# Value pages of four decode samples fetched in turn, their products issued in turn into four 32-column strips

## The reference

```python
k_prev = cache_k[j][page_table].reshape(Bs, PAST_LEN, H_A, DH_A)
v_prev = cache_v[j][page_table].reshape(Bs, PAST_LEN, H_A, DH_A)
...
s = jnp.einsum('bqhd,bqhjkd->bqhjk', qc.astype(F32), kg.astype(F32)) * scale
...
p = jax.nn.softmax(s.reshape(s.shape[:3] + (-1,)), axis=-1).reshape(s.shape)
return jnp.einsum('bqhjk,bqhjkd->bqhd', p, vg.astype(F32)).astype(q.dtype)
```

```python
S = S * g_chunk + jnp.einsum('bjhd,bjhe->bhde', kj * d_out, vj)
...
ob = head_rmsnorm(ob, ret_g) * jax.nn.silu(gb.astype(F32)).reshape(B, T, H_B, DV_B)
```

## Time and profile before

| what | value |
|---|---|
| median of 3 runs | 960.27 us (959.93 to 964.94) |
| span of the profiled execution | 959.2 us |
| PE busy | 883.4 us, 92% |
| DVE busy | 622.1 us, 65% |
| ACT busy | 420.1 us, 44% |
| value pages | 64 DMAs of 256 KB |
| page products (line 1604) | 128 matmul instructions |

### The profile page before, as it was taken

One profiled execution on the slowest core, in us unless ns is written; L12 is line 12 of the kernel. 1 busy time (PEld: TensorE's weight loads), 2 busy tenths in 40 slices (PEclk: granted clock), 3 DMA queues, 4 the chain that ended last, 5 costly groups with the idle time before them and its releaser, 6 DMA issues.

```text
span 959.2 us, 16875 instructions
## 1 busy us (share of the span) xinstructions
PE 883.4 (92%) x6145; PEld 761.0 (79%) x6145; DVE 622.1 (65%) x943; ACT 420.1 (44%) x695; POOL 257.4 (27%) x226
## 2 busy tenths in 40 slices
PE   2999894969999999999999999969969999999996
PEld 1988783742325999999999999857648999999995
DVE  3689988660032798888556656565476888887442
ACT  4434333341011565555545433564334655555442
POOL 6154767710100332232001000161221332222010
PEclk9999996588999999999999999975597999999997
DMA  9837675335565555554556667403353566653631
GB/s 275 284 129 242 199 260 183 128 94 160 192 220 175 176 177 175 178 184 129 172 177 192 191 187 216 161 10 100 88 155 93 171 192 188 188 157 121 183 119 46
DMA packets 154406, 159.83 MB, mean 167 GB/s; under 512 B 11793, under 2 KB 136349, under 8 KB 154335
## 3 DMA queue, kind: packets, MB, share of 16 engines
q1 hardware_dynamic: 145520, 151.09, 50.6%
q10 hardware_dynamic: 7966, 6.33, 2.2%
q0 software_dynamic: 864, 1.68, 0.7%
HBM read 150.76 MB, written 8.50 MB: 166 GB/s over the span
## 4 chain that ended last, share of the span: by engine, by line
PE 81%; DVE 11%; ACT 4%; issue 2%; DMA 2%; ACTq 0%; POOL 0%; SPq 0%; DVEq 0%
PE bank L1396 20%; PE bank L1397 20%; PE bank L1398 20%; PE bank L1604 6%; DVE w_lo L921 3%; DVE sc_all L973 2%; PE bank L1773 1%; PE bank L1726 1%; DMA z<-in_c_out_norm_g 1%; PE bank L1485 1%; PE bank L1600 1%; PE bank L1566 1%; PE bank L1748 1%; PE bank L1737 1%; DVE z L968 1%
## 5 line engine op out<-in xcount | busy, mean ns | idle before, releaser
L530 ACT ACTIVATE w_hi<-w_raw 128x1024 fp32r<-128x1024 f32 (+2 forms) x230 | 227.9, 993 | 297.8 <-PE bank L1398 294.5
L921 DVE TENSOR_TENSOR w_lo<-w_raw,w_hi 128x1024 fp32r<-128x1024 f32 (+2 forms) x230 | 296.1, 1289 | 83.6 <-ACT w_hi L530 83.4
L1396 PE MATMUL bank<-actB_hi,w_hi 128*128 128x264 f32 x704 | 200.1, 284 | 0.0
L1397 PE MATMUL bank<-actB_lo,w_hi 128*128 128x264 f32 x704 | 199.5, 283 | 0.0
L1398 PE MATMUL bank<-actB_hi,w_lo 128*128 128x264 f32 x704 | 199.3, 283 | 0.0
L1396 PE MATMUL bank<-actA_hi,w_hi 128*128 128x264 f32 x624 | 184.8, 296 | 5.8 <-DVE w_lo L921 2.9
L1397 PE MATMUL bank<-actA_lo,w_hi 128*128 128x264 f32 x624 | 180.1, 289 | 0.0
L1398 PE MATMUL bank<-actA_hi,w_lo 128*128 128x264 f32 x624 | 179.8, 288 | 0.0
L1397 PEld LDWEIGHTS bank<-actB_lo,w_hi 128*128 128x128 f32 x704 | 132.6, 188 | 0.1
L1396 PEld LDWEIGHTS bank<-actB_hi,w_hi 128*128 128x128 f32 x704 | 132.6, 188 | 0.1
L1398 PEld LDWEIGHTS bank<-actB_hi,w_lo 128*128 128x128 f32 x704 | 132.0, 187 | 0.0
(11 more groups left out here) (326 smaller groups left out, 1191.2 us busy)
## 6 DMA issues: line engine op xcount, KB each, us to landing
w_raw<-in_ffn_w SPq DMA_DIRECT2D x44, 1024.0 KB, 5.3
kv<-in_cache_k SPq DMA_DIRECT2D x64, 256.0 KB, 3.0
kv<-in_cache_v SPq DMA_DIRECT2D x64, 256.0 KB, 3.1
w_raw<-in_c_w_in SPq DMA_DIRECT2D x16, 1024.0 KB, 5.6
w_raw<-in_ab_w_in SPq DMA_DIRECT2D x14, 1024.0 KB, 5.4
w_raw<-in_ffn_w SPq DMA_DIRECT2D x16, 768.0 KB, 4.5
w_raw<-in_ffn_w SPq DMA_DIRECT2D x16, 640.0 KB, 4.1
w_raw<-in_ab_w_out SPq DMA_DIRECT2D x4, 1024.0 KB, 5.7
```

The costliest lines, as they stand in the source:

```text
L530: A(whi[u % RING][:, 0:nk, :], raw[u // 2 % RING][:, 0:nk, P * (u % 2):P * (u % 2) + P], ACT.Copy).then_inc(sem("hi_ready"), 1)
L921: V.tensor_tensor(wlo[u % RING][:, 0:nk, :], raw[u // 2 % RING][:, 0:nk, P * (u % 2):P * (u % 2) + P], whi[u % RING][:, 0:nk, :].bitcast(F ...
L1396: M(bank[b][:, 0:T], hi[:, k, :], src[0][:, k0 + k, :], start=first and k == 0, stop=False)
L1397: M(bank[b][:, 0:T], hi[:, k, :], src[1][:, k0 + k, :], start=False, stop=False)
```

## The change

The value pages are taken in another order, and SP loads their page numbers pair by pair. `v_page(v)` gives for the v-th fetch the sample, the pair within the sample, and the buffer: fetches 0 to 3 are the first pair of samples 0, 1, 2 and 3, in buffers 0 to 3; fetches 4 to 7 their second pair; from fetch 16 on come samples 4 to 7. PE goes through eight batches of four pairs. In a batch it waits for all four buffers, then issues eight page products, the first page of each of the four samples and then the second of each. Each sample's result lies in its own 32 rows of the bank, as before. The four products for the own token stand together ahead of batches 0 and 4. The retention work moves with `between`: two of its items behind each batch, and the last three behind the last batch.

```diff
--- before.py
+++ after.py
@@ -74,6 +74,11 @@
 JOBS1 = [(n, t, half) for n, t in (("q", 2), ("k", 2), ("v", 2), ("k", 0), ("k", 1), ("v", 0), ("v", 1)) for half in (0, 1)]
 CRING = 3
 EXP_MAX = 41.0
+
+
+def v_page(v):
+
+    return 4 * (v // 16) + v % 4, v // 4 % 4, v % 4
 
 
 def jobs_until(u):
@@ -290,6 +295,19 @@
 
                 page_pair(j, cache_k, (sem("k_reduced"), j - 3) if j >= 4 else None)
 
+            def v_pages(v):
+                b, pair, i = v_page(v)
+                at = NPAGE * b + 2 * pair
+                rows = nc.values_load_multi_w_load_instructions(
+                    pg[0:1, at:at + 2], engines=[mybir.EngineType.SP], min_val=0, max_val=NPOOL - 1)[1]
+                if v < 4:
+                    sp.wait_ge(sem("k_reduced"), 29 + v)
+                else:
+                    sp.wait_ge(sem("v_used"), v - 3)
+                for t in range(2):
+                    sp.dma_start(kv[i][:, t, :], cache_v[0, bass.ds(rows[t], 1)].rearrange("o p h d -> p (o h d)")
+                                 ).then_inc(sem(f"kv_landed{i}"), 16)
+
             for n in range(14):
                 load_raw(n, w_in0[:, :, 256 * n:256 * n + 256])
                 if n == 0:
@@ -310,9 +328,8 @@
                 k_pages(13 + 2 * n)
             for j in range(20, 32):
                 k_pages(j)
-            for j in range(32):
-
-                page_pair(j, cache_v, (sem("k_reduced"), 29 + j) if j < 4 else (sem("v_used"), j - 3))
+            for v in range(32):
+                v_pages(v)
 
             def ffn_loads(l, u_up, u_dn):
                 def pair(n, c, i8):
@@ -1593,22 +1610,31 @@
             claim(7, "samp_own", 2)
             pe.wait_ge(sem("own_p_diag"), 1)
             pe.wait_ge(sem("samp_pt_out"), 1)
-            for j in range(32):
-                b, r = j // 4, 32 * (j // 4 % 4)
-                out = bank[6 + b // 4][r:r + H, :]
-                if j % 4 == 0:
-                    M(out, dgp[:, b, :], tks["va"][:], start=True, stop=False)
-                pe.wait_ge(sem(f"kv_landed{j % 4}"), 32 * (8 + b + 1))
+            def between(n):
+                if n < 4:
+                    state_update(4 + n)
+                elif 5 <= n < 13:
+                    ret_o((n - 5) // 4, (n - 5) % 4)
+                elif 13 <= n < 17:
+                    ret_squares(n - 13)
+
+            for n in range(8):
+                q, pair = n // 4, n % 4
+                outs = [bank[6 + q][32 * i:32 * i + H, :] for i in range(4)]
+                if pair == 0:
+                    for i in range(4):
+                        M(outs[i], dgp[:, 4 * q + i, :], tks["va"][:], start=True, stop=False)
+                for i in range(4):
+                    pe.wait_ge(sem(f"kv_landed{i}"), 32 * (8 + n + 1))
                 for t in range(2):
-                    g = 2 * (j % 4) + t
-                    ins = M(out, pts[:, g, 8 * b:8 * b + 8], kv[j % 4][:, t, :], start=False, stop=g == NPAGE - 1)
-                ins.then_inc(sem("v_used"), 1)
-                if j < 4:
-                    state_update(4 + j)
-                elif 5 <= j < 13:
-                    ret_o((j - 5) // 4, (j - 5) % 4)
-                elif 15 <= j < 19:
-                    ret_squares(j - 15)
+                    g = 2 * pair + t
+                    for i in range(4):
+                        b = 4 * q + i
+                        ins = M(outs[i], pts[:, g, 8 * b:8 * b + 8], kv[i][:, t, :], start=False, stop=g == NPAGE - 1)
+                        if t == 1:
+                            ins.then_inc(sem("v_used"), 1)
+                for k in range(2 * n, 2 * n + 2) if n < 7 else (14, 15, 16):
+                    between(k)
             claim(5, "mix_lo", 5)
             pe.wait_ge(sem("samp_own"), 2)
             for t in range(2):
```

## The result

The changed kernel takes 991.84 us (median of 4 runs, 987.35 to 997.54), the kernel before 960.1 (4 runs, 959.9 to 964.94). The ratio is 1.0313 with a 95% interval of 1.0267 to 1.0359. The profiled execution has a span of 991.2 us against 959.2.

The account below looks back on a forecast made before the run. The prediction took the stage as bound by PE in series. Batches +18.7 us, tail +13.6 and clock +3.6 summed to +35.9 us, giving 996 us (chance 0.50); own range 986 to 1006, wider range 974 to 1016.

Parts of the forecast that it names:

- PE in series before the change, no page wait: Page-product stage of the kernel before: PE busy 81.61 of 81.65 us, with no wait for a page.
- Four strips side by side: A batch's 16 page instructions run as four in a row per strip: 1.74 us at full clock, 3.3 at half.
- The refill: From release of the four buffers until all four are filled again: 10.3 us, bounds about 8 and 12 us.
- The half clock: PE, idle between batches, loses its clock, so a batch's page products take 3.3 us.
- The batches: Seven batches of 13.6 us each after batch 0; the last page product ends 18.7 us later.
- The tail: Behind the last page product PE waits for VectorE's chain after three late squares: 13.6 us, 11.7 at full clock.
- 3.6 us for the clock: Half-clock cost behind the tail's idle: 1.9 us in line 1616's products and 1.7 us in the output projection.
- that term of 1.7 us: Start of the output projection: one more half-clock stretch of 3.4 us, in which 1.7 us is lost.
- strict order: Rival: products start strictly in order, nine steps or 7.5 us a batch at half clock; 1010 us, chance 0.14.
- no overlap: Rival: four strips do not overlap, 16 instructions in series, 8.7 us a batch; 1024 us, chance 0.13.
- the full clock: Rival: PE's clock stays full over the batches, 1.74 us of products each, period 12.0 us; 980 us, chance 0.20.
- Not slower: Rival: fetches run on through the products, stage at the transfers' rate, 7.5 us a batch; 950 us, chance 0.03.

Follow-up runs that it names:

- Experiment 2: The changed kernel with SyncE loading a batch's eight page numbers at once, in place of two ahead of each pair: 990.69 us, ratio 1.0251.
- experiment 4: The changed kernel with 16 unread products of constants behind each of batches 0 to 6, to keep PE busy: 985.96 us.
- experiments 10 and 11: Unaltered kernels run again: the changed kernel (10), 993.14 us, and the kernel before (11), 964.78 us.
- experiment 3: The changed kernel with PE issuing both products of one sample, then of the next, within a batch: 997.37 us, ratio 1.0347.
- experiments 7 and 8: The changed kernel with a second set of four page buffers (7), 951.17 us; that plus eight page numbers loaded at once and earlier squares (8), 943.85 us.
- experiment 9: The changed kernel with two buffer sets, eight page numbers at once and early squares, plus all retention items behind batches 0 to 3: 946.71 us.

## Why the prediction was right

*PE in series before the change, no page wait.* Right; all the time came from what the change added.

*Four strips side by side.* Right, at the bound that I took: 3.6 us for 16 instructions at half clock; 3.3 were taken, and the 0.3 us is mostly the last instruction's own length (1.06 us) beyond its step (0.85).

*The refill.* Sized at 10.3 us, measured 9.8 to 12.9, on average 10.7 (14.3 less 3.6). Of that PE stood idle 7.9 us a batch (55.5 over 7), more than the some 6 forecast. Batch 2's refill was the longest: two loads of the table took 1.11 and 1.35 us there in place of 0.47, and the landings up to 4.0. That term was too small because one load of the table, timed once, stood for all. Experiment 2 shows the issue chain, and that the transfer lies only 1.3 us beneath.

*The half clock.* Right for almost the whole stage (0.50 and 0.54); experiment 4 gives its price, 1.7 us a batch.

*The batches.* +18.7 us forecast, +24.0 measured in the profiled execution (E - S 81.65 and 105.67): 5.3 us too little, 0.7 us a batch and 0.3 us in batch 0.

*The tail.* Forecast 13.6 us and 3.6 us for the clock, measured 12.8 us in all (O - E 16.7 and 3.9), 4.4 less. PE in order of time, the three squares:

```profile
328.37 1.60 PE L1592 MATMUL bank<-z,cst 128*128 128x264 f32 x6
```

They ran at full clock, so they took 1.6 us and not 3.8. From the end of the last one to the take-out of the sums it is 9.8 us (329.97 to 339.74), as forecast. Line 1616's products cost 1.6 us more, where 1.9 was forecast. The projection lost nothing more than before, since before too it starts with 3.4 us at half clock; that term of 1.7 us was wrong by its own row.

So the sum was +35.9, and the stage measured +36.9: the batches cost 5.3 us more than forecast and the tail 4.4 less. That the two errors cancel is luck, and so is the single microsecond between the sums: experiments 10 and 11 have +30.2 for the same stage. What is borne out is the mechanism, both parts of it. The forecast time of 996 us is 4 us over the median. In the profiled executions the rest lies outside the stage: 36.9 + 5.9 - 10.8 = 32.0 us. I had taken the half-clock stretches elsewhere as fixed. Of the rivals, strict order and no overlap are out by experiment 3 and by the 3.6 us; the full clock held for no batch from start to end but could be had (experiment 4). "Not slower" is what experiments 7 and 8 make real, with the fifth to eighth buffer that it needed.

## What to carry over

A product order that needs several buffers at once also frees them at once: count the buffers before the products. Here the strips cut PE's work for a batch fourfold in steps, and the lock step of release, refill and products cost more than they gave; a second set of buffers turned +3% into -1.4%, and -2% with the two other edits. Taking a limit away brings the next one forward: with buffers enough, the rate at which the issuing engine loads page numbers and starts DMAs set the pace. When side work is rescheduled around a loop, follow what stands behind it on the in-order engine: three small products behind the loop cost 11 to 13 us of the stage. And compare stages, not only medians, where stretches at half clock last differently in each execution.

## What the runs showed of the hardware

- Four column strips of 32 with 512 float32 columns each ran fully side by side (16 instructions in 3.6 us at a granted clock of 0.50, 1.9 us at 1.00), and the two orders of issue that were tried took the same time (3.58 us with all of one strip in a row).
- Page numbers into SyncE's registers: a load of two took 0.47 us as a rule (up to 1.80), of eight side by side in the table 0.53 us (the kernel before), of eight in four places of two 1.7 to 2.1 us in every case (experiments 2, 8 and 9).
- With unaltered code the half-clock stretch of the mLSTM stage was 61.4 or 51.2 us (before) and 41.0 or 51.2 us (after), and with the same code in that stage 20.5 us in experiment 9; the time behind the attention stage followed it, from 637.5 us at 20.5 to 656.8 at 61.4.
